# Attention rounds one unit sooner, and other start offsets for the activation tiles of a two-block transformer kernel

## What is computed

```python
h = rms_norm(x, g_mix[layer])
qkv = h @ w_in[layer]                      # 1024 -> 3072
# 16 heads of 64: differential (4), causal (4), dilated (8), each with a partial rotation
mix = concatenate([o_a, o_b, o_c], axis=-1)
x = x + mix @ w_out[layer]
h2 = rms_norm(x, g_ffn[layer])
u = causal_conv3(h2 @ w_up[layer]) + conv_b   # 1024 -> 5632
gate, val = split(u, 2)
x = x + (silu(gate) * val) @ w_down[layer]
```

## Time and profile before

| | us |
|---|---|
| median of 3 runs | 1717.65 |
| lowest, highest | 1716.96, 1717.94 |
| the profiled execution | 1717.02 |
| its span | 1715.2 |
| PE busy | 1677.6 (98%) |
| DVE busy | 1162.7 (68%) |
| ACT busy | 822.0 (48%) |
| POOL busy | 705.3 (41%) |

### The profile page before, as it was taken

How to read it: one execution, slowest core, us unless ns; L and a number is a source line. 1 busy time by engine, 2 the same in 40 slices (tenths; PEclk the granted TensorE clock), 3 DMA queues, 4 the chain that set the end, 5 groups by cost and what they waited for, 6 DMA issues and landing times.

```text
span 1715.2 us, 27184 instructions
## 1 busy us (share of the span) xinstructions
PE 1677.6 (98%) x10701; PEld 1457.1 (85%) x10701; DVE 1162.7 (68%) x2430; ACT 822.0 (48%) x1458; POOL 705.3 (41%) x386
## 2 busy tenths in 40 slices
PE   7999999999999999999999999999999999999998
PEld 6779998787799986545599999999999988888886
DVE  6656776766477586665453999999999644444444
ACT  5555665454576642113353454544444454455544
POOL 3424676143266821521255899500000144444443
PEclk9999999999999999999999999999999999999999
DMA  8333546463155464333364556544444566666663
GB/s 299 116 107 135 192 159 206 147 232 123 50 204 203 171 197 146 105 97 122 108 244 139 185 172 191 175 140 145 139 146 137 163 218 193 190 195 195 196 193 126
DMA packets 77599, 283.20 MB, mean 165 GB/s; under 512 B 8736, under 2 KB 8992, under 8 KB 77216
## 3 DMA queue, kind: packets, MB, share of 16 engines
q1 hardware_dynamic: 76032, 276.24, 49.5%
q10 hardware_dynamic: 1440, 5.23, 0.8%
HBM read 279.33 MB, written 2.10 MB: 164 GB/s over the span
## 4 chain that ended last, share of the span: by engine, by line
PE 89%; DVE 4%; POOL 3%; ACT 2%; issue 1%; DMA 0%; POOLq 0%; ACTq 0%; DVEq 0%
PE bank L564 72%; PE bank L555 8%; PE bank L619 5%; POOL wl L2213 2%; PE bank L877 1%; PE bank L1019 1%; PE bank L687 1%; PE bank L932 1%; ACT wh L1172 1%; DVE xs L1543 1%; DVE mix L1582 0%; ACT att L1175 0%; DVE headtmp L1543 0%; PE bank L580 0%; PE bank L707 0%
## 5 line engine op out<-in xcount | busy, mean ns | idle before, releaser
L2213 POOL TENSOR_TENSOR wl<-raw,wh 128x1024 fp32r<-128x1024 f32 x209 | 540.2, 2593 | 672.9 <-ACT wh L1172 660.8
L564 PE MATMUL bank<-hh,wh 128*128 128x256 f32 x1856 | 525.2, 283 | 3.6 <-POOL wl L2213 2.7
L564 PE MATMUL bank<-hl,wh 128*128 128x256 f32 x1856 | 518.2, 279 | 0.0
L564 PE MATMUL bank<-hh,wl 128*128 128x256 f32 x1856 | 518.0, 279 | 0.0
L1172 ACT ACTIVATE wh<-raw 128x1024 fp32r<-128x1024 f32 x476 | 491.7, 1050 | 52.6 <-PE bank L564 39.7
L1537 DVE TENSOR_TENSOR wl<-raw,wh 128x1024 fp32r<-128x1024 f32 x267 | 367.6, 1385 | 80.5 <-ACT wh L1172 79.9
L564 PEld LDWEIGHTS bank<-hh,wh 128*128 128x128 f32 x1856 | 348.6, 188 | 4.4 <-POOL wl L2213 3.4
L564 PEld LDWEIGHTS bank<-hh,wl 128*128 128x128 f32 x1856 | 348.3, 188 | 0.0
L564 PEld LDWEIGHTS bank<-hl,wh 128*128 128x128 f32 x1856 | 348.0, 188 | 0.0
L1543 DVE TENSOR_TENSOR acl<-H,ach 128x256 fp32r<-128x256 f32 x128 | 87.6, 685 | 181.5 <-ACT ach L1175 181.5
L564 PE MATMUL bank<-wh,ach 128*128 128x512 f32 x512 | 199.4, 389 | 0.8 <-DVE acl L1543 0.8
(11 more groups left out here) (218 smaller groups left out, 2305.3 us busy)
## 6 DMA issues: line engine op xcount, KB each, us to landing
raw<-in_ut_dram SPq DMA_DIRECT2D x128, 512.0 KB, 3.5
raw<-in_vt_dram SPq DMA_DIRECT2D x128, 512.0 KB, 3.6
raw<-in_wup_dram SPq DMA_DIRECT2D x88, 512.0 KB, 4.0
raw<-in_win_dram SPq DMA_DIRECT2D x48, 512.0 KB, 4.6
raw<-in_wdown_dram SPq DMA_DIRECT2D x44, 512.0 KB, 4.2
raw<-in_wout_dram SPq DMA_DIRECT2D x24, 512.0 KB, 3.6
raw<-in_wga_dram SPq DMA_DIRECT2D x16, 512.0 KB, 3.5
raw<-in_wpq_dram SPq DMA_DIRECT2D x16, 512.0 KB, 4.9
```

What stands on the lines that cost most here:

```text
L564: m = p.e.matmul(out, lhs[i][a], rhs[i][b], start=start and i == 0 and j == 0, stop=stop and i == n - 1 and j == 2)
L2213: g.e.tensor_tensor(low_of(u), raw_of(u), high_of(u).bitcast(F32), ALU.subtract).then_inc(pool_lo.up(("lo", u)), 1)
```

## The change

Two edits in constants. First, the places of the rounds and of two turns among the units: rounds 1 to 7 stand behind units 9, 11, 13, 15, 17, 19, 21 instead of 10, 12, ..., 22; rounds 0 and 8 keep units 8 and 23; turns 6 and 10 stand behind units 14 and 18 instead of 15 and 19. All of PE, DVE and ACT read these tables. Second, the tile of activations in `hh` and `hl` begins at column 14, 18 or 20 (56, 72 or 80 bytes) in layer 0, layer 1 and the second block, where it began at column 16 (64 bytes) in all three.

```diff
         def hT_of(st):
-            o = 16 if st[0] == "f" else 0
+            o = {("f", 0): 14, ("f", 1): 18, ("f", 2): 20}.get(st, 0)
             return [w[:, o:o + 2048].rearrange("p (k t) -> p k t", k=8) for w in (hh, hl)]
...
-        QUADS = {**{8 + 2 * m: m for m in range(8)}, 23: 8}
+        QUADS = {8: 0, **{7 + 2 * m: m for m in range(1, 9)}}
...
-        QK_TURNS = [{8 if L == 0 else 7: (0, 2), 13: (4, ), 15: (6, ), 17: (8, ), 19: (10, )} for L in range(DEPTH)]
+        QK_TURNS = [{8 if L == 0 else 7: (0, 2), 13: (4, ), 14: (6, ), 17: (8, ), 18: (10, )} for L in range(DEPTH)]
```

## The result

| | us |
|---|---|
| before, median of 6 runs (lowest, highest) | 1717.34 (1713.88, 1718.56) |
| after, median of 6 runs (lowest, highest) | 1725.39 (1722.78, 1728.79) |
| ratio, with its 95% interval | 1.0052 (1.0042 to 1.0062) |
| the profiled execution of after, its span | 1728.79, 1727.0 |

The kernel became slower by 0.52%, which is 8 to 9 us (the two medians are 8.05 us apart). The forecast was 1712.0 us with a range of 1705 to 1716, so it is wrong in sign. Rival D, which had a chance of 0.06, gave 1723.7.

What follows compares the result with a forecast made beforehand. The prediction took PE to bound the kernel, busy 1677.6 of 1715.2 us. Terms -6.1 + 0.5 + 0.3 - 0.3 = -5.6 us, offsets 0, took 1717.65 to 1712.0 us; 8-in-10 range 1705 to 1716.

Steps and rivals of the forecast that it cites:

- Rival D: 256-column stages: weight loads and streamed columns meet in memory, 2.1 ns a product, +11.7 us, time 1723.7; chance 0.06.
- the offsets: 256-column stages: new activation tile starts taken to cost 0 us, bounded by -24.5 and +3.9 us.
- rival C: Only the up projections lose, each product reading one 16-byte piece more: +3.9 us, time 1715.9; chance 0.08.
- Step 1: Input projections: rounds 2, 4, 6 behind a slab's last unit remove five PE waits for DVE's copy; gain 6.1 us.
- rival A: Waits return elsewhere and hold PE at the next round; half the gain is lost, leaving 2.8 us, time 1714.9; chance 0.15.
- point 5: DVE's last step of `difference(0)` newly waits for Pool's root; costed at nothing, up to 3 us per layer without cover.
- steps 2 and 3: Turn of unit 13 waits for Pool's rotation, +0.5 us; round 1's transposes in layer 1 wait, +0.3 us.
- step 4: Turns 4 and 8 now stand next to a round, saving switches between product kinds; 0.3 us gain for both layers.
- Step 5: DVE's last step of `difference(0)`, in round 4, newly waits for Pool's root; costed at nothing.

Runs made afterwards that it cites:

- a1_rounds: Only the moved rounds and two turns against the kernel before, activation tiles at 64 bytes as before; 1714.58 us, ratio 0.9983.
- a3_by64: Rounds as before, activation tiles at 0, 128 and 256 bytes in layer 0, layer 1 and the second block; 1727.85 us.
- a4_by16: Rounds as before, activation tiles at 16, 32 and 48 bytes in layer 0, layer 1 and the second block; 1720.11 us.
- c2_sweep: Rounds as before, activation tiles at 24, 40 and 96 bytes in layer 0, layer 1 and the second block; 1732.61 us.
- a2_offsets: Only the new offsets (56, 72, 80 bytes) against the kernel before, rounds as before; 1728.59 us, ratio 1.0070.
- b2_weights_shifted: Rounds as before, weight tiles 64 bytes later, activations at 64, 96 and 128 bytes, so distances of 0, 32 and 64; 1723.23 us.
- b3_swapped: Rounds as before, the change's offsets dealt out otherwise: 80, 56, 72 bytes in layer 0, layer 1, second block; 1729.16 us.
- c1_rounds_unit: Moved rounds, tiles at 64 bytes, and low part of layer 0's unit 16 on DVE instead of POOL; 1711.03 us against 1717.07 before, ratio 0.9963.
- b4_all32_unit: Moved rounds, all tiles at 32 bytes, and low part of layer 0's unit 16 on DVE instead of POOL; 1711.74 us, ratio 0.9963 against before.

## Why the prediction was wrong

**The failed step is the offsets, "I take 0, since the weight loads, which do not move, fill the time by themselves".** They cost 11.3 us in the trace of after and 11.4 in the run of the offsets alone. The reading behind it was the 110.00 of 110.00 us of weight loads in the earlier trace rows. But the record of one load is 188 ns long in the stages of either kind (the mean of the page for the 256-column and for the 512-column groups). Where products start 117.8 ns apart, such records overlap each other and the share is full whatever sets the pace; where they start 226.2 ns apart it must be 188 / 226.2 = 83%, which is the 165.62 of 200 us. The contrast in which I saw a limit is what this record length gives by itself.

**The bounds missed as well.** My upper bound, +3.9 us (rival C), was a price of the 16-byte piece for the two up projections only; these alone lost 6.4 us, and the second block 4.9. Rival D, that loads and streamed columns get in each other's way by where they lie, is the mechanism that the runs bear out. Its +2.1 ns a product came from the excess of the 512-column rows at distance 0; measured were +2.2, +3.8, +2.2 and +1.6 ns. That the sizes are so close is in part luck: the price was one of distance 0, which none of the new tiles had, and with the weights moved by 64 bytes the 512-column products went the other way than the 256-column ones. Even so, I had this rival's price and left it out of both the upper bound and the range. From 1.0 ns a product on it turned the sign of the whole change, and there was no row against it; 0.06 was too little for a case with nothing against it but an argument on a busy share.

**The two rules.** The 16-byte lines of the Trainium skill, "Advanced Engine Details and Errata" ("Memory Cachelines") spare 80 bytes and would make 0 and 256 good; all three run at 120.0 ns, so they don't explain the pace. "TensorE: Matmul & The Clock Gate" of the Trainium skill, Part 2, lets loads and the stream read without slowing each other, with 109 ns by its issue gap as an estimate. The runs don't agree: no distance measured here reached it. The lowest pace was 113.3 ns, most lay between 116.7 and 121.5, and it changed with the distance between the two tiles.

**Step 1 (five waits go, -6.1 us).** Right for four of five. The fifth, the largest, went from 1.86 to 2.44 us. The text looked at what stood before the copy as rounds alone; the constants' piece of layer 0 and POOL's subtraction, which followed ACT to an earlier place, were not in it. The long wait was followed by some 3.4 us at half clock, where eight products from 58.22 to 61.20 start 0.425 us apart instead of 0.226: 8 x 0.2 = 1.6 us. The wait and this stretch are why layer 0 gained 0.4 us instead of 3.7; in a1_rounds the stretch was 6.8 us long and layer 0's rounds took 72.24 us, more than before. The stretch doesn't need the meeting, though. With the rounds as before and a wait of 1.8 to 1.9 us at this place, three kernels (a3_by64, a4_by16, c2_sweep) had 3.5 us at half clock from 54 or 55 us on, and rounds of 72.6 to 72.7 us; four others (before, a2_offsets, b2_weights_shifted, b3_swapped) had none, and 71.5. All three with the wait of 2.44 us had it, neither of the two with 0.23 us. The rounds alone gained 2.6 us, which is close to the 2.8 of rival A, but not for its reasons: neither the step of point 5 nor the rotation held PE.

**Steps 2 to 4.** With the meeting away (c1_rounds_unit) steps 2 and 3 can be read by themselves. PE waits 0.33 us at the turn of unit 13, where I had put 0.4 to 1.1 and before it was 0.20: the cost is 0.1, not 0.5. What it waits for is not what I took it for. These are the turn, the end of the rotation, and ACT's last copy of that round out of a bank, in c1_rounds_unit; the last line is the same copy in before:

```profile
60.27 0.65 PE L730 MATMUL bank<-ids,qkv 128*128 128x128 f32 x4 [0.33 <-ACT att L1175]
57.28 1.03 POOL L2218 TENSOR_TENSOR qkv<-mix 128x128 f32<-128x128 f32 x2
59.85 0.36 ACT L1175 ACTIVATE att<-bank 128x256 f32<-128x256 f32 x1
...
61.36 0.36 ACT L1175 ACTIVATE att<-bank 128x256 f32<-128x256 f32 x1
```

The rotation is over at 58.31, some 2 us before the turn. The turn starts 0.06 us after ACT's copy ends at 60.21, and before the change it started at 61.77, 0.05 us after that copy ended at 61.72. So ACT, which the profile named and which I called done, was the one awaited. My sum of the arrival was off too: 1.86 and 0.2 make 2.1 us, not 2.3, and PE's last product ahead of the turn ends at 59.94. The rotation itself began at 54.14 and not at about 55.4, as POOL no longer had the low part before it; with it, in after, 56.69. In layer 1 the transposes of round 1 follow the scores with no wait, where I had 0.3 us; step 4, the 0.3 us of gain, was not measured by itself (timeline of PE in after):

```profile
370.67 0.71 PE L555 MATMUL bank<-qkT 32*128 32x128 f32 x8
371.32 0.66 PE L687 MATMUL bank<-ids,att 128*128 128x128 f32 x4
371.73 0.47 PE L564 MATMUL bank<-wh,hh 128*128 128x512 f32 x1
```

The rounds of layer 1 took 2.16 us less, against 1.9 by the prediction (two waits of 1.6, 0.4 for their ends, 0.15 for the switches, less 0.3). The sum of both layers in c1_rounds_unit is 3.50 + 2.16 = 5.7 us, the span fell by 5.7 and the median by 6.0: the -5.6 of the rounds was the right size, with the one low part out of the way. That it fits to 0.1 us is luck, as its parts were off by up to 0.4.

**Step 5 (DVE's new wait).** Right. In after DVE stood for the root (timeline of DVE), and no wait of PE was left there:

```profile
77.79 0.42 DVE L1543 TENSOR_TENSOR headtmp<-headtmp,sml 128x256 f32<-128x256 f32 x1
80.21 0.43 DVE L1543 TENSOR_TENSOR mix<-headtmp,sta 128x256 f32<-128x256 f32 x1 [2.00 <-POOL sta L2218]
```

**What was not foreseen at all** is the 2.75 us of half clock near 717 us. It is in no stage of either edit. Of the other kernels, a2_offsets had a stretch of 3.4 us at 670.9, b2_weights_shifted one at 439.6, and c2_sweep three, one of which is 6.8 us long and lies at 720.0, as in after; before, b3_swapped, b4_all32_unit and c1_rounds_unit had none until their last microseconds. Executions of every kernel here differ by a few microseconds with their mean clock (0.996 to 0.999 in runs of before), so I take it as scatter, not as an effect of the change. Whether the change makes such stretches likelier was not settled.

## What to carry to other kernels

A busy share of 100% on two overlapping units doesn't say which one sets the pace: work out from the rows what one instruction would need alone, and treat a pace above it as something that a layout may move either way. Where a tile's place in memory changes, put both ends of the paces that the trace does show on every product concerned, and let the range hold them. Where work is moved on one engine, list everything that stands before the awaited instruction in that stretch, one-time pieces too, and see which operation of the neighbour now runs beside it.

## What the runs showed of the hardware

- A product of 256 columns with a load of weights of 128 columns beside it starts every 113.3 to 121.5 ns at full clock, by the distance in bytes between the starts of the two tiles, each counted within its own buffer: 0: 120.0; 16: 118.7; 24: 119.9; 32: 116.7 to 117.9; 40: 119.1; 48: 118.4; 56: 118.2 or 120.0; 64: 117.8, seldom 113.3; 72: 121.5; 80: 120.0, in places 118.5; 96: 120.0; 128: 118.7; 256: 120.0. No simple rule was found in it, and most of these distances ran once.
- The pace is constant over dozens of units and then jumps to another fixed value (117.8 to 113.3 at 64 bytes, 117.8 to 116.9 at 32), so each distance has several stable patterns. What picks one was not found; no run tried to.
- With 64 bytes between the tiles instead of 0, products of 256 columns gained 2.2 ns (activations streamed); products of 512 columns lost 2.1 ns (weights streamed, and moved by 64 bytes; one run).
- An operation of DVE on 128 x 16 numbers took 2.35 us instead of 0.17 beside a subtraction of POOL of the same length, in three kernels.
- Around the first product of unit 12 in layer 0, with a PE wait of 2.44 us there, the granted clock was at half for 3.4 to 6.8 us in three of three kernels; with one of 1.8 to 1.9 us in three of seven; with one of 0.23 us in none of two. A stretch of 3.5 us there cost about 1.2 us (rounds of 72.6 to 72.7 us against 71.5).
